# Second block's out and down projections: the high and the low activations in one 512-column product

## The reference, cut to what matters

```
merged = sigmoid(gate_attn) * (attn @ w_branch_attn) + sigmoid(gate_ssm) * (ssm @ w_branch_ssm)
x = x + merged @ w_out                                   # w_out: 2048 x 2048
h = rms_norm(x, ffn_norm_g)
val, gate = split(h @ w_up, 2)                           # w_up: 2048 x 11264
x = x + (val * gelu(conv(gate))) @ w_down                # w_down: 5632 x 2048
return rms_norm(x, final_norm_g)
```

## Time and profile before

| | |
|---|---|
| three timed runs | 2674.3, 2674.31 and 2671.6 us; median 2674.3 |
| span of the profiled execution | 2672.7 us |
| time of the profiled execution beyond its span | the profile gives the span alone; the median of the timed runs is 1.6 us above it |
| TensorE busy | 2642.9 us, 99% of the span, 22834 products |
| VectorE busy | 1804.4 us, 68% |
| ScalarE busy | 1274.7 us, 48% |
| read from HBM | 492.57 MB, 185 GB/s over the span |

### The profile page before, as it was taken

The page is one execution under the profiler, slowest core; times in us unless marked ns, Lnnn a source line. Parts: engine busy times, 40 slices in busy tenths (PEclk is TensorE's granted clock), DMA queues, the critical chain, the costliest instruction groups (busy, mean ns, idle before and its releaser), DMA issues.

```text
span 2672.7 us, 57540 instructions
## 1 busy us (share of the span) xinstructions
PE 2642.9 (99%) x22834; PEld 2628.9 (98%) x22834; DVE 1804.4 (68%) x2269; ACT 1274.7 (48%) x1548; POOL 249.9 (9%) x206
## 2 busy tenths in 40 slices
PE   9999999999999999999999999999999999999998
PEld 9999999999999999999999999999999999999998
DVE  5455555747888888864467999867576777775444
ACT  5334455345344444444455556554455555554442
POOL 1000000030000000001101665400100000000000
PEclk9999999999999999999999999999999999999999
DMA  7665556574555655556656555556656666666664
GB/s 256 193 199 175 150 161 182 169 213 148 173 195 196 196 194 189 196 191 203 192 168 200 174 163 157 155 183 200 194 183 195 196 194 193 191 190 197 195 191 141
DMA packets 137806, 496.71 MB, mean 186 GB/s; under 512 B 15425, under 2 KB 15425, under 8 KB 137537
## 3 DMA queue, kind: packets, MB, share of 16 engines
q1 hardware_dynamic: 137520, 494.20, 59.7%
q10 hardware_dynamic: 144, 0.52, 0.1%
HBM read 492.57 MB, written 2.10 MB: 185 GB/s over the span
## 4 chain that ended last, share of the span: by engine, by line
PE 89%; DVE 6%; DVEq 2%; ACT 1%; DMA 1%; issue 1%; ACTq 0%; SPq 0%
PE bank L432 86%; DVE w_lo L982 2%; PE ps_a L432 1%; PE ps_o L432 1%; PE ps_n L432 1%; DVE act_lo L1021 1%; PE ps_t L432 0%; DMA hT<-in_xT 0%; ACT w_hi L676 0%; DMA w_raw<-in_w_in 0%; ACT act_hi L742 0%; DVE hT L1046 0%; DVE pr L1309 0%; DVE rstd L1005 0%; DVEq L1299 0%
## 5 line engine op out<-in xcount | busy, mean ns | idle before, releaser
L982 DVE TENSOR_TENSOR w_lo<-w_raw,w_hi 128x1024 fp32r<-128x1024 f32 x928 | 1134.1, 1234 | 720.8 <-ACT w_hi L676 719.2
L676 ACT ACTIVATE w_hi<-w_raw 128x1024 fp32r<-128x1024 f32 x928 | 977.0, 1056 | 1185.9 <-PE bank L432 1045.3
L432 PE MATMUL bank<-act_hi,w_hi 128*128 128x256 f32 x5408 | 1275.3, 279 | 3.0 <-DVE gate_y L1350 2.5
L432 PE MATMUL bank<-act_lo,w_hi 128*128 128x256 f32 x5408 | 1264.9, 277 | 0.0
L432 PEld LDWEIGHTS bank<-act_hi,w_hi 128*128 128x128 f32 x5408 | 1014.9, 188 | 4.1 <-issue 2.7
L432 PEld LDWEIGHTS bank<-act_lo,w_hi 128*128 128x128 f32 x5408 | 1015.7, 188 | 0.7
L432 PE MATMUL bank<-act_hi,w_lo 128*128 128x256 f32 x5408 | 726.9, 277 | 2.7 <-DVE w_lo L982 2.7
L432 PEld LDWEIGHTS bank<-act_hi,w_lo 128*128 128x128 f32 x5408 | 666.6, 188 | 3.1 <-DVE w_lo L982 3.1
L432 PE MATMUL bank<-f_lo,w_hi 128*128 128x256 f32 x1408 | 327.9, 276 | 0.0
L432 PE MATMUL bank<-f_hi,w_hi 128*128 128x256 f32 x1408 | 327.9, 276 | 0.0
L432 PEld LDWEIGHTS bank<-f_lo,w_hi 128*128 128x128 f32 x1408 | 264.3, 188 | 0.0
(11 more groups left out here) (227 smaller groups left out, 1790.3 us busy)
## 6 DMA issues: line engine op xcount, KB each, us to landing
w_raw<-in_w_up SPq DMA_DIRECT2D x352, 512.0 KB, 4.2
w_raw<-in_w_in SPq DMA_DIRECT2D x252, 512.0 KB, 4.2
w_raw<-in_w_down SPq DMA_DIRECT2D x176, 512.0 KB, 4.2
w_raw<-in_w_out SPq DMA_DIRECT2D x64, 512.0 KB, 4.4
w_raw<-in_w_ple_gate SPq DMA_DIRECT2D x32, 512.0 KB, 4.5
w_raw<-in_w_branch_attn SPq DMA_DIRECT2D x16, 512.0 KB, 3.9
w_raw<-in_w_branch_a SPq DMA_DIRECT2D x8, 512.0 KB, 4.1
w_raw<-in_w_branch_b SPq DMA_DIRECT2D x8, 512.0 KB, 3.5
```

Of the source, the lines that this page charges most:

```text
L432: return pe.matmul(o, l, r, start=start, stop=stop, skip_group_check=True)
L676: act.activation(w_hi[:, k, 0:n, :], w_raw[:, k, 0:n, :], ACT.Copy).then_inc(hi_ready, 1)
L982: dve.tensor_tensor(w_lo[:, k, 0:n, :], w_raw[:, k, 0:n, :], w_hi[:, k, 0:n, :].bitcast(F32), ALU.subtract).then_inc(lo_ready, 1)
```

## The change

For `out2` and `down2` alone (`st.halves`), the two products with w_hi become one of 512 columns. For that the high and the low activations are put in one buffer with a leading index of 2 (`act_x`, `f_x`, and in the same way `y_x`, `p_x`, `x2_x`), and `both[:, :, x, :]` reads 256 high and 256 low columns. The two halves c of the features no longer fit in one bank. PSUM is laid out as two `twin` tensors of two banks each: half c goes to bank c of the twin, with the product by high activations in its first 256 columns and the one by low activations in its last 256. The w_lo products are added to the first 256. `bank` and `ps_a` are now names for the two banks of a twin. The DVE adds the two halves of each bank to hT one after the other.

```
-        act_hi = sb("act_hi", [P, DT, TOK], F32R)
-        act_lo = sb("act_lo", [P, DT, TOK], F32R)
+        act_x = sb("act_x", [P, 2, DT, TOK], F32R)
+        act_hi, act_lo = act_x[:, 0, :, :], act_x[:, 1, :, :]
...
+        twin = [ctx.enter_context(nc.psum_tensor(f"twin{i}", [P, 2, 2, TOK], F32)) for i in range(2)]
+        bank = [t[:, 0, :, :].rearrange("p h t -> p (h t)") for t in twin]
+        ps_a = [t[:, 1, :, :].rearrange("p h t -> p (h t)") for t in twin]
...
+        st_out2.halves = st_down2.halves = True
...
+        def halves_of(st, s):
+            of = twin[(st.group0 + s) % 2]
+            return of[:, :, 0, :], of[:, :, 1, :]
...
                                 w = w_hi[:, k, t, c * P:(c + 1) * P]
+                                if st.halves:
+                                    mm(twin[(st.group0 + s) % 2][:, c, :, :], w, both[:, :, x, :], j == 0 and t == 0, False)
+                                    continue
                                 mm(o, w, xh[:, x, :], j == 0 and t == 0 and c == 0, False)
                                 mm(o, w, xl[:, x, :], False, False)
...
-                                last = mm(ps[:, c * TOK:(c + 1) * TOK], w_lo[:, k, t, c * P:(c + 1) * P],
+                                o = halves_of(st, s)[0][:, c, :] if st.halves else ps[:, c * TOK:(c + 1) * TOK]
+                                last = mm(o, w_lo[:, k, t, c * P:(c + 1) * P],
...
-                    dve.tensor_tensor(h, h, bank_of(st, i, s)[:, :].rearrange("p (c t) -> p c t", c=2),
-                                      ALU.add).then_inc(evacuated["dve"], 1)
+                    of_hi, of_lo = halves_of(st, s)
+                    dve.tensor_tensor(h, h, of_hi, ALU.add)
+                    dve.drain()
+                    dve.tensor_tensor(h, h, of_lo, ALU.add).then_inc(evacuated["dve"], 1)
```

More of the change, by code:

```diff
@@ L103, in __init__ @@
         self.written_out = 1
+        self.halves = False
         self.pieces = [-(-kt // PIECE_KT) for _, _, kt, _ in slots]
@@ L201, in build @@
         z_b, t_b, l_b, sp_b, lw_b = over(80 * T, *((n, [P, BLK]) for n in ("z_b", "t_b", "l_b", "sp_b", "lw_b")))
-        y_hi, y_lo = over(KA * T, ("y_hi", [P, 8, T], F32R), ("y_lo", [P, 8, T], F32R))
+        y_x, = over(KA * T, ("y_x", [P, 2, 8, T], F32R))
+        y_hi, y_lo = y_x[:, 0, :, :], y_x[:, 1, :, :]
         mT, eT, tmp, sg, sq_x = over(
@@ L213, in build @@
         sq_sum = lambda n: squares_of(n)[:, 4:6, :]
[L215 to L218, removed]
+        f_x, gate_y, gate_g, val_y = over(
+            0, ("f_x", [P, 2, FT, T], F32R), ("gate_y", [P, 2, T]), ("gate_g", [P, 2, T]), ("val_y", [P, 2, T]))
+        f_hi, f_lo = f_x[:, 0, :, :], f_x[:, 1, :, :]
+        p_x, = over(2 * FT * T, ("p_x", [P, 2, 2, T], F32R))
+        p_hi, p_lo = p_x[:, 0, :, :], p_x[:, 1, :, :]
         proj2, kpad, vpad, s2_buf, small2, bc_pad, cz, rot, turns, vrot, scn, xs, pr, cz_t = over(
@@ L228, in build @@
         turn_t = tab[:, 2 * BLK + T:2 * BLK + 3 * T].rearrange("p (k t) -> p k t", k=2)
[L230 to L235, removed]
+        x2_x, glu_v, glu_g = over(
+            PROJ2 * T, ("x2_x", [P, 2, 16, T], F32R), ("glu_v", [P, 4, T]), ("glu_g", [P, 4, T]))
+        x2_hi, x2_lo = x2_x[:, 0, :, :], x2_x[:, 1, :, :]
+        twin = [ctx.enter_context(nc.psum_tensor(f"twin{i}", [P, 2, 2, TOK], F32)) for i in range(2)]
+        bank = [t[:, 0, :, :].rearrange("p h t -> p (h t)") for t in twin]
+        ps_a = [t[:, 1, :, :].rearrange("p h t -> p (h t)") for t in twin]
         ps_t = [ctx.enter_context(nc.psum_tensor(f"ps_t{i}", [P, 512], F32)) for i in range(2)]
@@ L284, in main_x @@
             return lambda j: (split_ready, first + j + 1)
-        act_x, f_x, p_x = (act_hi, act_lo), (f_hi, f_lo), (p_hi, p_lo)
         G = GROUP
@@ L306, in build @@
                         2, act_x, None, "dve")
-        st_branch = Stage("branch", branch1, 4, (y_hi, y_lo), lambda j: (split_ready, SPLIT["y1"] + 2), "dve")
+        st_branch = Stage("branch", branch1, 4, y_x, lambda j: (split_ready, SPLIT["y1"] + 2), "dve")
         st_out = Stage("out", pair("w_out"), 4, act_x, main_x(SPLIT["merged"]), "act")
@@ L316, in build @@
         st_in2b = Stage("in2b", tiles("w_in_2", ORDER_2[20:21]), 1, act_x, None, "dve")
-        st_glu = Stage("glu", [cols("w_glu_2", 4, 8, 0, k * G) for k in range(4)], 1, (x2_hi, x2_lo),
+        st_glu = Stage("glu", [cols("w_glu_2", 4, 8, 0, k * G) for k in range(4)], 1, x2_x,
                        lambda j: (split_ready, SPLIT["ssm_y"] + 1), "act")
         st_in2c = Stage("in2c", tiles("w_in_2", ORDER_2[21:]), 1, act_x, None, "dve")
-        st_branch2 = Stage("branch2", branch2, 2, (x2_hi, x2_lo), lambda j: (split_ready, SPLIT["ssm"] + 1), "dve")
+        st_branch2 = Stage("branch2", branch2, 2, x2_x, lambda j: (split_ready, SPLIT["ssm"] + 1), "dve")
         st_out2 = Stage("out2", pair("w_out_2"), 4, act_x, main_x(SPLIT["merged2"]), "dve")
@@ L434, in stream @@
             def stream(st, beside=None):
-                xh, xl = st.x
+                both, xh, xl = st.x, st.x[:, 0, :, :], st.x[:, 1, :, :]
                 def body(i, first):
```

## The result

The changed kernel takes 2676.92 us (median of 9 runs, 2674.97 to 2679.31) against 2671.6 us for the kernel before (9 runs, 2669.4 to 2674.35). The ratio is 1.0021 with a 95% interval of 1.0012 to 1.0030: some 5.6 us slower, between 3.2 and 8.0. The forecast was 2672.3 us and no change; slower had a chance of 0.1. It started from 2674.3, the median of the first three of the nine runs before, and the nine have 2671.6.

A forecast was written before the change was run, and what follows sets the result against it. TensorE, busy 99% of the span, was taken as the bound. Products -6.2, final add +0.8, longer wait +1.7 and clock loss +1.7 gave -2.0 us, from 2674.3 to 2672.3 us, range 2666 to 2678.

The forecast's parts named there:

- merged product: In out2 and down2, one 512-column product replacing two of 256 would take 215.7 ns, against 226.7 for the two.
- w_lo product behind it: In out2 and down2, the 8 w_lo products per piece would slow from 113.3 to 117.8 ns, losing 36 ns a piece.
- wait at up2's second piece: TensorE's wait for DVE between out2 and up2 would grow from 0.55 to 2.3 us, costing 1.7 us.
- clock lost behind the wait: After the 2.3 us wait in up2, TensorE would more likely than not drop to half clock, costing 1.7 us.
- second add at the end: DVE's extra add before the last store has nothing to hide it, costing 0.8 us.
- the price of a 512-column product: Step pricing the long product in out2 and down2 at 215.7 ns, saving 11.0 each, 10.6 us over 960.
- the float32 rows: Trace rows at 1484.80 us: four float32 products of 256 columns, 512 clocks each, at 215.6 ns, used as price stand-in.
- what is not columns stays with every 256 columns: Rival for out2 and down2: long products cost 224.2 ns, w_lo products still slow; +5.9 us, 2680.2 us; chance 0.12.
- The w_lo term: In out2 and down2, w_lo products behind long products would go at 117.8 ns, cutting the saving to 6.2 us.
- slow pace: Full-clock float32r products at about 118 instead of 113.3 ns, seen after float32 or half-clock products, expected throughout out2 and down2.
- The second rival: In out2 and down2, w_lo products keep 113.3 ns; 2668.1 us with clock loss, 2666.4 without; chance 0.2.
- The second add: DVE's evacuations end 0.77 us later, hidden inside stages; shows from out2 to up2 (+1.7 us) and at the end (+0.8).

The follow-up runs named there:

- e1: Changed kernel with high and low activations of a tile adjacent in down2, so each product reads one run of 512 columns; 2677.96 us, ratio 1.0021 to the kernel before.
- e7: Changed kernel with each merged product reading 128 high and 128 low columns, 256 in all; 113.3 ns a product, 118 ns further on.
- e14: Changed kernel with down2's merged products reading one fixed place of 512 float32r columns, 4 bytes apart; 228 ns a product.
- e10: Changed kernel with down2's merged products reading 512 packed bfloat16 constants, weights also bfloat16; 217 ns a product, 216 behind the first step.
- e13: Changed kernel with out2's merged product replaced by a 256-column float32 product of the high activations alone, added twice; 216 ns a pass.
- e2: Changed kernel with a piece's 8 merged products reordered, four per feature half, so four in a row write one bank; 229 ns a product, single run 2674.49 us.
- e5: Kernel before, with out2 and down2 adding each group twice to the residual, a drain between; 2675.13 against 2671.98 us, ratio 1.0007.
- e8: Changed kernel with down2's merged products reading weights and activations as bfloat16 from the upper halves of the float32r words; 227 ns a product.
- e4: Changed kernel with each merged product reading 192 high and 192 low columns, 384 in all; 174 ns a product.
- e12: Changed kernel with each merged product reading 160 high and 160 low columns, 320 in all; 147 ns a product.

## Why the prediction was wrong

The size of the loss follows from five terms of the sum, each against what it measured:

| term | predicted | measured | difference x count |
|---|---|---|---|
| merged product | 215.7 ns | 229.4 ns | +13.7 ns x 960 = +13.2 us |
| w_lo product behind it | 117.8 ns | 113.95 ns | -3.85 ns x 960 = -3.7 us |
| wait at up2's second piece | +1.7 us | +1.4 us | -0.3 us |
| clock lost behind the wait | +1.7 us | 0 | -1.7 us |
| second add at the end | +0.8 us | +0.7 us | -0.1 us |

From the forecast sum of -2.0 us these lead to +5.4 us, where the medians give +5.3.

The 2676.92 us lie inside the stated range of 2666 to 2678, but that is luck: the range was set out from 2674.3, and the kernel before came in 2.7 us lower. From 2674.3, +5.3 would have been 2679.6.

- **The step that failed** is "the price of a 512-column product". I read the 6.6 ns beyond 256 columns at 2.4 GHz as a charge on the product and took the float32 rows for a product's price at 512 clocks. The charge grows with the columns that are read, when these are 4 bytes apart: 6.6 ns for 256 and 16.1 for 512, in one run of columns or two (e1, e7, e14), and only 2.5 for 512 packed ones (e10). The float32 rows could not show it, because such a pass reads half as many columns in its time (e13). The rival that had this mechanism, "what is not columns stays with every 256 columns", put the product at 224.2 ns and was given 0.12. Its reason, two runs far apart and two banks in turn, was wrong (e1, e2). Its sum of +5.9 us is close to the measured +5.3 by luck: it has the product 5.2 ns too low (5.0 us), the w_lo products 3.7 us too high, and 1.7 us for a clock loss that did not come.
- **The w_lo term** had the right observation and the wrong case. The slow pace follows products of 216 ns (e10), but of those of 229 only the first w_lo product is slow. As the product was mis-priced, this term fell with it. The second rival had these products at 113.3 ns, which they kept, but its reason, long products that leave time for the loads, is not borne out: those of 216 ns in e10 leave nearly as much, and the slow pace comes. In the earlier trace rows I had taken "the array was the slower party" for the condition, and did not ask whether a float32r product of 512 columns is like the float32 ones in this.
- **The second add** was right at both places, in mechanism and nearly in size. 0.55 us and two times 0.76 make the 2.07 us of e5; in the changed kernel TensorE also comes 4 x 0.03 us later, which leaves the 1.96, where the forecast had it come 0.2 earlier. It was hidden inside the stages, as said; e5 has it alone.
- **The clock** stayed. In all the profiled executions with two adds and pieces of 2.69 to 2.75 us (the changed kernel, e1, e2, e5, e8, e10 and e14), the wait was 1.96 to 2.07 us and the clock was kept. Where the shorter pieces made the wait at this place 3.7 us (e4, e12), the clock was lost behind it, and in e7 behind waits of 3.1 and 2.2 us. Of the waits elsewhere, the one of 2.5 us lost it in 11 of the 13 profiled executions and the one of 2.0 to 2.1 in 7 of 13. So the length of a wait alone does not decide it here, and why the seven at this place all kept it stays open. I had weighed two waits of one execution as if they were a rule.
- **What stays open:** why products longer than 256 columns exceed the line by 2.7 to 5.6 ns, how much of that is the slow pace, and what starts and ends that pace; and whether e10's constants have a part in its 216 ns.

## What to carry to other kernels

Before paying for fewer and longer products, find out whether the distance between products is a charge on each product or on each column: two lengths of the same kind of product tell, if both go at the same pace, and one length never does. A stand-in row must be alike in what it reads per clock, not only in how long it holds the array. And a reordering that gains nothing on the busy engine still pays for its by-products, here a second dependent add at every hand-over that has no cover.

## What the runs showed of the hardware

- Moving columns 4 bytes apart pass at 113.3 ns for 256 (float32r) at the full granted clock, which is 17/16 of a clock at 2.4 GHz each, and at 229.4 ns for 512; bfloat16 picked from float32 words takes 225 to 227 ns for 512 (e8). Packed bfloat16 columns take 215.7 ns for 512 (e10). The Trainium skill (TensorE: Matmul & The Clock Gate, "Back-to-back issue gap") gives columns / 2.4 GHz + 2.5 ns for the gap of a single product, 215.8 for 512: the packed columns agree, the ones 4 bytes apart do not.
- At the half clock the charge is gone: 213 ns for 256 columns.
- How often an execution loses the clock behind the same waits differs from run to run, and the time of a run follows it. In 36 runs of the kernel before the nine with a mean granted clock of 0.997 take 2669.6 to 2671.8 us and the eight with 0.995 take 2673.3 to 2675.4. The means of the two are 3.5 us apart, of a spread of 5.8 us over all 36.
